# Spacing the weight slots of a three-pass transformer-layer kernel by 4 and by 32 bytes

## The reference

```python
hx = modulate(rms_norm(x, g_mix_pre), sh1, sc1)          # 512 tokens; the context alike, 256 tokens
uf_x, xc_x, ug_x = mixer_inputs(hx, w_in, conv_w, conv_b) # h @ w_in, 2048 -> 3072, conv of 4 taps
hf_x, hb_x = bi_rglru(xc_x, *lru_p, hf_c[:, -1], hb_c[:, 0])
y_x = mixer_output(uf_x, hf_x, hb_x, ug_x, w_f, b_f, w_out)   # 2-D DFT per group, 2048 -> 2048
x = x + gt1 * rms_norm(y_x, g_mix_post)
hx2 = modulate(rms_norm(x, g_ffn_pre), sh2, sc2)
x = x + gt2 * rms_norm(conv_ffn(hx2, w_up, conv_w, conv_b, w_down), g_ffn_post)   # 2048 -> 2*5632 -> 2048
```

## Time and profile before

| | |
|---|---|
| median of three runs | 2122.01 us (2117.51 to 2125.58) |
| profiled execution, span from the first to the last instruction | 2116.7 us |
| PE busy | 2084.5 us, 98% |
| PEld busy | 1772.6 us, 84% |
| DVE busy | 1529.5 us, 72% |
| ACT busy | 811.8 us, 38% |
| granted TensorE clock, mean | 0.995 |
| DMA | 311.19 MB, mean 147 GB/s |

### The profile page before, as it was taken

How to read it: one execution, slowest core, us unless ns; L and a number is a source line. 1 busy time by engine, 2 the same in 40 slices (tenths; PEclk the granted TensorE clock), 3 DMA queues, 4 the chain that set the end, 5 groups by cost and what they waited for, 6 DMA issues and landing times.

```text
span 2116.7 us, 28297 instructions
## 1 busy us (share of the span) xinstructions
PE 2084.5 (98%) x11682; PEld 1772.6 (84%) x11682; DVE 1529.5 (72%) x2202; ACT 811.8 (38%) x1077; POOL 78.6 (4%) x145
## 2 busy tenths in 40 slices
PE   7999999999999999999999999999999999999998
PEld 4678887898777888989889898888988889888887
DVE  5567878867988975867667676676766758577577
ACT  5247667543323442423324233332333424233243
POOL 0000000001110000000000000000000000000002
PEclk9999999999999999999999999999999999999999
DMA  9953424435876424333333433333333343233343
GB/s 393 408 198 111 158 100 152 147 95 202 305 284 218 163 94 136 100 130 110 110 122 106 132 100 114 122 103 130 100 119 120 100 129 100 90 100 100 100 172 107
DMA packets 86193, 311.19 MB, mean 147 GB/s; under 512 B 9456, under 2 KB 13552, under 8 KB 84016
## 3 DMA queue, kind: packets, MB, share of 16 engines
q1 hardware_dynamic: 67824, 243.09, 33.6%
q0 software_dynamic: 17424, 65.50, 9.3%
q10 hardware_dynamic: 816, 0.79, 0.1%
HBM read 300.95 MB, written 8.39 MB: 146 GB/s over the span
## 4 chain that ended last, share of the span: by engine, by line
PE 69%; DVE 2%; DMA 1%; issue 0%; ACT 0%; DVEq 0%; ACTq 0%
PE bank L987 23%; PE bank L989 23%; PE bank L988 23%; DMA ada_raw<-in_adabg 1%; DVE w_lo L1531 0%; DMA x<-in_adabg 0%; DVE acc L2166 0%; PE bank L1098 0%; PE bank L1283 0%; DVE ada_acc L1563 0%; DMA w_raw<-in_stream 0%; DVE x L1871 0%; DVE prod L1882 0%; DVE ss L1539 0%; DVE acc L2138 0%
## 5 line engine op out<-in xcount | busy, mean ns | idle before, releaser
L987 PE MATMUL bank<-h_hi,w_hi 128*128 128x512 f32 (+1 forms) x1968 | 711.6, 362 | 3.9 <-DVE w_lo L1531 1.6
L988 PE MATMUL bank<-h_lo,w_hi 128*128 128x512 f32 (+1 forms) x1968 | 708.8, 360 | 0.0
L989 PE MATMUL bank<-h_hi,w_lo 128*128 128x512 f32 (+1 forms) x1968 | 707.0, 359 | 0.0
L1531 DVE TENSOR_TENSOR w_lo<-w_raw,w_hi 128x1024 fp32r<-128x1024 f32 x260 | 315.9, 1221 | 160.5 <-ACT w_hi L601 160.4
L601 ACT ACTIVATE w_hi<-w_raw 128x1024 fp32r<-128x1024 f32 x260 | 273.1, 1056 | 399.3 <-DMA w_raw<-in_stream 399.3
L987 PEld LDWEIGHTS bank<-h_hi,w_hi 128*128 128x128 f32 x1968 | 372.3, 189 | 63.5 <-issue 11.6
L989 PEld LDWEIGHTS bank<-h_hi,w_lo 128*128 128x128 f32 x1968 | 372.2, 189 | 56.8
L988 PEld LDWEIGHTS bank<-h_lo,w_hi 128*128 128x128 f32 x1968 | 372.5, 189 | 49.1
L987 PE MATMUL bank<-act_hi,w_hi 128*128 128x512 f32 (+1 forms) x688 | 268.8, 391 | 1.6 <-DVE acc L2138 1.5
L989 PE MATMUL bank<-act_hi,w_lo 128*128 128x512 f32 (+1 forms) x688 | 268.1, 390 | 0.0
L988 PE MATMUL bank<-act_lo,w_hi 128*128 128x512 f32 (+1 forms) x688 | 268.0, 390 | 0.0
(11 more groups left out here) (340 smaller groups left out, 2710.2 us busy)
## 6 DMA issues: line engine op xcount, KB each, us to landing
w_raw<-in_stream SPq DMA_DIRECT2D x340, 512.0 KB, 3.5
ada_raw<-in_adabg POOLq DMA_DIRECT2D x112, 512.0 KB, 4.5
ada_raw<-in_ada SPq DMA_DIRECT2D x64, 512.0 KB, 13.8
x<-in_x_t SPq DMA_DIRECT2D x4, 1024.0 KB, 8.6
acc<-in_adabg SPq DMA_DIRECT2D x8, 512.0 KB, 5.8
x<-in_x_t POOLq DMA_DIRECT2D x4, 1024.0 KB, 8.6
x_kept_d<-x SPq DMA_DIRECT2D x4, 1024.0 KB, 5.6
c<-in_ctx_t SPq DMA_DIRECT2D x2, 1024.0 KB, 14.4
```

What stands on the lines that cost most here:

```text
L987: t.matmul(out, w, v, start=start, stop=False)
L988: t.matmul(out, w, v_l, start=False, stop=False)
L989: return t.matmul(out, w_l, v, start=False, stop=stop)
L1531: v.tensor_tensor(lo_unit(n), raw_unit(n), hi_unit(n).bitcast(F32), ALU.subtract).then_inc(lo_done, 1)
```

## The change

Two constants are added and the slots get that many elements more. `w_raw` and `w_lo` have 1032 elements a slot (4128 bytes), `w_hi` 1025 (4100 bytes). The unit that is used is still the first 1024 elements of a slot. `ada_rows` is no buffer of its own any more but the first half of `csq0`.

```diff
+PAD_HI, PAD_LO = 1, 8
...
-        w_raw, w_lo = twice(ctx, "w_raw", "w_lo", [P, RING, UNIT])
-        w_hi = sbuf(ctx, "w_hi", [P, RING, UNIT], F32R)
+        w_raw, w_lo = twice(ctx, "w_raw", "w_lo", [P, RING, UNIT + PAD_LO])
+        w_hi = sbuf(ctx, "w_hi", [P, RING, UNIT + PAD_HI], F32R)
...
-                ada_rows = sbuf(s0, "ada_rows", [P, 2 * P])
+                ada_rows = csq0[:, 0, :]
...
         def raw_unit(n):
             if n < UNITS - KEPT:
-                return w_raw[:, SLOT[n], :]
+                return w_raw[:, SLOT[n], 0:UNIT]
...
-                return w_hi[:, SLOT[n], :]
+                return w_hi[:, SLOT[n], 0:UNIT]
...
-                return w_lo[:, SLOT[n], :]
+                return w_lo[:, SLOT[n], 0:UNIT]
...
-                a.activation(ada_rows[:, :], rows_bank(c)[:, 0:2 * P], ACT.Copy).then_inc(rows_copied, 1)
+                a.activation(ada_rows, rows_bank(c)[:, 0:2 * P], ACT.Copy).then_inc(rows_copied, 1)
```

## The result

The changed kernel takes 2131.46 us, the median of 11 runs (2124.75 to 2133.32). The kernel before, run beside it, has 2117.99 us, also over 11 runs (2115.39 to 2125.58), so its earlier median of three, 2122.01, was 4 us high. The two medians lie 13.5 us apart. The ratio, taken over all these runs, is 1.0051 with an interval of 1.0039 to 1.0063: the change costs half a per cent, 10.8 us. That is just above the 10.6 us that the prediction took as the least that can be told from nothing, and the interval leaves out 1. Forecast were 2131 us, +9.6 us on the execution profiled.

What follows compares the result with a forecast made beforehand. PE was taken as the bound, 98% busy: number of matmuls times start-to-start distance. Terms 16.5 - 2.4 - 4.5 = +9.6 us on a 2116.7 us span gave 2126.3, plus 5.3 to the median: 2131 us, range 2098 to 2146.

Steps and rivals of the forecast that it cites:

- 1: 512-column matmuls of `h` by `w`: lose the state in step, 227.1 to 232 ns each, +16.5 us after hiding.
- The cover: Output projection, 500 to 625 us: DVE's and the DMA's chain ends last, hiding 2.3 us of slower `h` matmuls.
- 2: Down-projection, 1968 matmuls of `act` by `w`: out of step before and probably after, 233.2 to 232 ns, -2.4 us.
- 3: 2640 matmuls of 256 columns on `h` and `t`: from 120.0 to about 118.3 ns, -4.5 us.
- 4: ACT writes and DVE reads `w_hi` off 16-byte multiples: 2 us on DVE, up to 11 on ACT, none on the path.
- 5: DMAs into `w_raw` start 32 bytes later with each slot: 0, up to 2 us in the first stage.
- 6: `ada_rows` in `csq0`: eight copies of 383 ns with the same waits, 0.
- A: Distances do nothing, the down-projection is slow for another reason: 2122 us, chance 0.17.
- B: `h` matmuls of 512 columns: misaligned, drifting distances cost more, 234 ns each, +23 us, 2145 us; chance 0.20.
- C: New distances are better: `h` stays at 227 ns, `act` falls to 226.7, -17 us, 2105 us; chance 0.30.

Runs made afterwards that it cites:

- the scans: Two kernels of matmul groups alone, no layer computed: weights' distance from tokens varied, first both together, then high and low separately; 1652.48 and 2191.59 us.
- e5: Kernel before, unpadded, with one gap of 128 bytes ahead of `act_hi`, so `act` is at distance 0 to the weights; 2106.92 us, ratio 0.9948.
- the first scan: PE alone, no layer computed: groups of 24 matmuls, both weights at one distance from the tokens, 0 to 508 bytes in steps of 4; 1652.48 us.
- e1: Against the kernel before, only the high weights' slots padded, by 4 bytes each; 2122.5 us, ratio 1.0019.
- e6: Kernel before, unpadded, with 192 bytes more behind `w_hi` and 192 more ahead of `act_hi`; 2099.19 us, ratio 0.9904.
- e2: Against the kernel before, only raw and low slots padded, by 32 bytes each, which puts the high weights' buffer 160 bytes later; 2130.17 us, ratio 1.0048.

## Why the prediction was right

The time came out as forecast (2131 against 2131.46), and by the mechanism that it named. By its own steps:

1. `h` by `w`: forecast +16.5, found +15.2. The price was 232 ns, found 231.2 and 231.9, and 11.11 us for the run of 48 where 11.1 was forecast. Right. The cover inside it was not there: 2.3 us were to be hidden in the output projection, but the 500 to 625 stretch grew by 2.3 us, 2.0 of it in these steps. So without the cover the term was +18.8, and its price was too high: I had 227.1 to 232, 4.9 ns, and over all 4177 steps on `h` it is 227.8 to 231.4, 3.6 ns. Two errors of 2.3 and 3.6 us cancelled in part.
2. `act` by `w`: forecast -2.4, found +0.4. This was the term with the wrong sign, on the idea that new distances are average ones. With the new distances the mean is 232.5 ns for high and 235.0 for low weights; the scans show that single distances lie anywhere from 226.7 to 237.6 with 512 columns, so a mean is no forecast for one.
3. 256 columns: forecast -4.5, found -4.7. Right, and the scan says why: distance 0 is in step but above the mean of 118.3 there.
4. ACT and DVE at addresses off 16 bytes: forecast 0, found 1 ns on DVE and 0 on ACT. Right.
5. and 6. The DMAs of `w_raw` land 3.5 us after issue (median) in both kernels. The eight copies of conditioning rows take 383 ns each before and 383 or 384 after, and PE's weight loads wait 4.1 us in all for them in both. The first 100 us have the same row as before within 0.2 us of PE's busy time. Right.

The forecast's base was off the other way. It added 5.3 us for the difference of the span to the median of three runs; with 11 runs that median is 1.3 us above the span of 2116.7. So the base was 4.0 us too high, and the difference too low: +9.6 us were forecast, the medians lie 13.5 us apart, and the ratio gives 10.8. That the time came out to half a microsecond is luck; the difference itself was forecast to 1 us by the ratio and to 4 by the medians, and its terms to 4 us (the price of the first one was that far off). On the spans the sum, 2126.3, compares with 2124.4 measured. With the 3.0 us of low clock taken out of the trace of before, the +9.6 us compare with 10.7 in place of 7.7.

Of the rivals, A (nothing changes, 2122 us) falls with e5. B (misaligned starts, 2145 us) falls with the first scan and e1: the mean did pass its 230 ns, but not because of starts inside a line. C (new distances are better, 2105 us) did not happen here; it would have needed five slots with a good distance each, and the scan has eight good ones in 64. As an idea it was the best of the three: e6 is C with distances that were chosen.

The Trainium skill has in "SBUF — State Buffer", section "Who interferes with whom", that PE never waits on anyone and that its two read ports are independent. The runs disagree with what would follow, that distances are free: the same two streams cost 226.8 or 237.6 ns in the scan with no other engine at work, by the distance of their addresses alone. A cost for starts inside a line, which the prediction worked out from the same page's box on SBUF "cachelines", was not seen: 231.3 to 232.9 ns by class, with 231.7 for the aligned one, between them. (The prediction's remark that the trace has no weight load that starts inside a line holds for loads of 128 columns; those of `csil`, two columns wide, start 8 bytes apart.)

One thing stays argued. The distance was moved on both sides and the steps followed it, but no run leaves the weight loads out, so it is not shown by itself that it is the load of a block beside the matmul that disturbs the stream of tokens.

## What to carry to other kernels

When PE is never idle, measure the distance from one matmul's start to the next, by kind of operand; equal shapes with unequal steps point to addresses. Lay out the streamed operand and the weights so that their starts agree modulo 256 bytes for 512 columns (every block is then in step); padding a weight slot by as little as 4 bytes undoes it. For 256 columns 0 is not the best distance, but no distance was found that is good in every surrounding: 64 bytes gave 113.7 or 118.0 ns in the scans and 115.3 to 118.6 in the kernel, so measure it in place. The gain was 1% here with two 192-byte gaps. To see effects of this size, sum the steps over the trace and time the kernel several times, since single executions of the same kernel differed by up to 10 us, half a per cent.

## What the runs showed of the hardware

- The commonest settled steps are whole multiples of 6.67 ns: 226.7 is 34, 233.3 is 35, 120.0 is 18 and 113.3 is 17. At a granted clock of 1.00 (2.4 GHz) that is 16 cycles. Over half of the 64 distances with 512 columns settle at one of the first two; with 256 columns most settle elsewhere (118.3, the mean, is no multiple). Why it is 16 no run shows.
- Even in step no group of 512 columns with weight loads beside it settled under 226.6 ns, though 512 cycles at 2.4 GHz are 213.3.
- The cost has a period of 256 bytes of distance, and 4 bytes are enough to lose the step (226.7 ns at 0, 232.0 settled at 4). What in the memory makes it stays open; no run here can tell.
- The step took five matmuls to settle at the start of the run of the earlier trace rows (230, 236, 229, 232, 231 ns, then 226 to 227), and so its 48 have a mean of 227.1.
- At 1.2 GHz the distance costs nothing that shows. In e2, with the weights 160 (high) and 128 (low) bytes off, seven steps in a fall of the clock take 426 or 427 ns each, which is 512 cycles at 1.2 GHz, and the 17 right behind it, at 2.4 GHz, take 3.96 us, 232.9 ns each. In the kernel before, at distance 0, six steps at 1.2 GHz (from 42.59 us) take 426 or 427 ns as well. So the loss, and the 13 ns over 512 cycles that even the matmuls in step have, are seen only at the higher clock. The rows of e2:

```profile
568.07 0.63 PE L989 MATMUL bank<-h_lo,w_hi 128*128 128x512 f32 x1
...
571.05 0.55 PE L990 MATMUL bank<-h_hi,w_lo 128*128 128x512 f32 x1
571.44 0.39 PE L988 MATMUL bank<-h_hi,w_hi 128*128 128x512 f32 x1
...
575.40 0.39 PE L990 MATMUL bank<-h_hi,w_lo 128*128 128x512 f32 x1
```
